# Prompt attention: maxima and sums copied to 64 columns by GpSimd and spread by two full-width products a block

## The chip, the cores and the metric

The kernel runs on one core of a Trainium2 chip. The metric is device time of one execution, in microseconds (us), as the median of several runs. Engines are called as in the profile: PE is TensorE (PEld its weight loads), DVE is VectorE, ACT is ScalarE, POOL is GpSimd, SP is SyncE, which here issues DMAs.

## The reference

One inference step of a trunk with two layers: an RWKV-7 layer and a layer of dilated sliding-window attention, each followed by a gated ConvFFN. Everything is float32. The prompt has 1024 tokens, the samples 64. What matters here is the attention of the prompt in three head groups with (window, dilation) = (128, 1), (512, 4), (2048, 16):

```python
sc = jnp.einsum('bdnqhe,bdnkhe->bdnqhk', qb, kb) * ATT_SCALE
sc = jnp.where(valid, sc, -jnp.inf)
lse = jax.nn.logsumexp(sc, axis=-1)
pr = jnp.exp(sc - lse[..., None])
o = jnp.einsum('bdnqhk,bdnkhe->bdnqhe', pr, vb)
...
wts = jax.nn.softmax(jnp.stack(lses), axis=0)
o = jnp.sum(wts[..., None] * jnp.stack(outs), axis=0)
```

So for each query and head the kernel needs, beside the weighted values, the maximum and the sum of its exponentials. They join the three groups in the end.

## The kernel before

`prompt_attention` works through 12 slots. A slot is one pair of heads (i = 0 to 3) in one head group (g = 0 to 2), in the order (0,0), (0,1), (0,2), (1,0) and so on. A slot has 8 blocks of 128 queries, and a block is handled for both heads of the pair, each with 64 channels.

The order on PE is written out by hand. The loop over a slot s has ten steps, n = 0 to 9. In step n PE issues `scores(s, n)` (for n < 8), a first part of the projections of slot s + 1 (`advance(s + 1, n, 0)`), `turn(s, n - 1)` (transposes of the exponentials), a second part of the projections (`advance(s + 1, n, 1)`) and `values(s, n - 2)`. Which pieces of the next slot's projections go into which step stands in `STEPS`: rotations rK and V products in steps 6 to 8, and in step 9 only the transposes T of V. The last slot, 11, has no next slot, so its steps hold attention alone.

`values(s, n)` writes one PSUM bank, `ps[:, 7]`: columns 0 to 127 get the weighted values (L2645 for the earlier key block, where there is one, and L2648 for the block's own), columns 128 to 255 the negated maxima, columns 256 to 383 the sums. Maxima `nm` and sums `zz` lie in SBUF with the query on the partition, one column a head. Line L2652 spreads such a column over 64 channels: its stationary operand is the column repeated 64 times (a broadcast read), its moving operand the 128 x 128 identity, its output 64 partitions x 128 queries. It is issued four times a block (2 quantities x 2 heads), each with 128 rows and 64 columns of the array. The last of them raises `nfull`; DVE then copies all 384 columns out (L2808) and raises `ntaken`.

The shapes of the array on PE around it: scores (L2618) use 64 rows and 128 columns (written 64\*128 in the profile), values and spreading 128 rows and 64 columns (128\*64), the projections (L2545, L2566), rotations (L2576), transposes of exponentials (L2630) and T in groups 0 and 1 (L2587) use 128\*128, T in group 2 (L2589) 128\*64. In float32 each product is two instructions on PE, and so two rows of a count.

The softmax of a block: DVE scales and masks (L2796), then takes the negated maximum (L2800); ACT forms the exponentials with the sum as a by-product, one head at a time (L2701), and raises `expd`; PE transposes them (L2630); ACT copies them out (L2711).

POOL in this function builds sums of weights for the projections, four additions of 128 x 512 a slot (L2524 to L2529), once the DMA has brought the slot's weights and PE has used the ones before; behind the loop it clears two regions for the sampled attention (L2531, L2533). In the slots 3, 6 and 9 DVE also joins the three groups of the previous pair (`later.merge`, L2346 to L2366, 128 x 1024 each, among them a reciprocal at L2363).

SP issues the weights of the next slots, the stores, and towards the end the loads and masks of the sampled attention (L2321, L2329, L2323). The block of `sampled_attention` begins when all engines have ended this one.

`tail` is called twice, once a layer. Its first product waits for the output weights by two semaphores.

Of the kernel before, what the change touches and what calls it, by code (L numbers as in the profile page):

```python
# [8 lines left out]
ALU = mybir.AluOpType  # L9
# [4 lines left out]
P = 128  # L14
# [42 lines left out]
    return region[:, start:start + count * width].rearrange("p (n w) -> p n w", w=width)  # L57


def tail(m, a, layer, src, kt, weights, mixed, middle, reload=None, save=None, early=None):  # L60

    nc = m.nc
    PADW = SEQ + 2 + NB * (NS + 2)
# [55 lines left out]

    with ExitStack() as ctx:  # L120
        sem = lambda n: ctx.enter_context(nc.semaphore(f"t{layer}_{n}"))
        wo_first, wo_rest = early if early is not None else (sem("wo_first"), sem("wo_rest"))
        xin = sem("xin") if reload is not None else None
        wup = [[sem(f"wup{s}{q}") for q in range(2)] for s in range(2)]
        vin = [sem(f"vec{s}") for s in range(2)]
# [87 lines left out]

        @block.sync
        def _(sp):
            if early is None:
                sp.dma_start(wot[:, 0], weights[0]).then_inc(wo_first, 16)
                sp.dma_start(wot[:, 1:KT], weights[1:KT].rearrange("n p k c -> p n k c")).then_inc(wo_rest, 16)
            if reload is not None:
                sp.dma_start(m.X, reload).then_inc(xin, 16)  # L220

            def keep_rows(f):

                sp.wait_ge(kept, f * 2 + 2)
                for q in range(2):
                    sp.dma_start(a["o_conv"][layer, f + q * FT], last2[:, 2 * (f % 2) + q, :]).then_inc(rows_out[f % 2], 16)

            for f in range(FT):
                s = f % 2
                if f == 2:  # L230
                    for b, (t0, n) in enumerate(TB):
                        sp.wait_ge(added, KT * (b + 1))
                        sp.dma_start(middle[:, :, t0:t0 + n], m.X[:, :, t0:t0 + n]).then_inc(m.x_moved, 16)
                for q in range(2):
                    if f >= 2:
                        sp.wait_ge(up, last_up(f - 2, q))
                    sp.dma_start(wt[s][q], a["wup"][layer, q * FT + f]).then_inc(wup[s][q], 16)
                if f >= 2:
                    keep_rows(f - 2)
                    sp.wait_ge(hidden, f - 1)  # L240
                sp.dma_start(vec[:, s, :], a["ffv"][layer, f]).then_inc(vin[s], 16)
            def part_in(n, q, r, dst, signal):
                sp.dma_start(dst, a["wdown"][layer, 2 * (n % 4) + q, :, r * HF:(r + 1) * HF, :]).then_inc(signal, 16)

            def keep_block(b):
                if b < 2:
                    sp.wait_ge(added, NU + KT * (b + 1))
                    rows = XIN[b]
                else:
                    if b == 3:  # L250
                        sp.wait_ge(conv, CONVS + 4)
                    sp.wait_ge(added, NU + (3 * KT if b == 2 else 3 * KT + 4))
                    rows = XS[b - 2]
                if save is not None:
                    sp.dma_start(save[:, :, DB[b]:DB[b] + PIECE], rows).then_inc(m.x_moved, 16)
                else:
                    sp.dma_start(a["o_y"][:, :, DB[b]:DB[b] + PIECE], rows).then_inc(y_out, 16)

            sp.wait_ge(up, last_up(FT - 2, 1))
            part_in(0, 0, 0, W11, a11_in)  # L260
            keep_rows(FT - 2)
            sp.wait_ge(conv, CONVS - 2)
            part_in(0, 1, 0, W21, a21_in)
            sp.wait_ge(up, at[FT - 1, 0, 2])
            part_in(0, 0, 1, W12, a12_in)
            sp.wait_ge(up, at[FT - 1, 1, 2])
            part_in(0, 1, 1, W22, a22_in)
            sp.wait_ge(m.x_moved, stored)
            sp.dma_start(m.H[:, :, HALF:T], middle[:, :, 0:HALF]).then_inc(m.x_moved, 16)
            keep_rows(FT - 1)  # L270
            for n in range(1, NDOWN):
                sp.wait_ge(product, down(n - 1, "P7"))
                part_in(n, 0, 0, W11, a11_in)
                if n == 5:
                    sp.wait_ge(m.x_moved, stored + 16)
                    sp.dma_start(hid[:, KT:2 * KT, 0:HALF], middle[:, :, HALF:T]).then_inc(m.x_moved, 16)
                sp.wait_ge(product, down(n - 1, "P5"))
                part_in(n, 1, 0, W21, a21_in)
                sp.wait_ge(sums_done, WSUMS + 4 * n)
                part_in(n, 0, 1, W12, a12_in)  # L280
                sp.wait_ge(product, down(n - 1, "P4"))
                part_in(n, 1, 1, W22, a22_in)
                if n == 5:
                    sp.wait_ge(m.x_moved, stored + 32)
                    keep_block(0)
                if n == 6:
                    keep_block(1)
                    if save is not None:
                        sp.wait_ge(m.x_moved, stored + 64)
            keep_block(2)  # L290
            keep_block(3)
            if save is not None:
                sp.wait_ge(m.x_moved, stored + 96)
            else:
                sp.wait_ge(y_out, 64)
            for s in range(2):
                sp.wait_ge(rows_out[s], FT * 16)

        @block.tensor
        def _(pe):  # L300
# [6 lines left out]
            def mixer(b, k):  # L307
                u = KT * b + k
                t0, n = TB[b]
                begun = early is not None and u < EARLY  # L310
                if early is not None:
                    pe.wait_ge(wo_first if begun else wo_rest, 16 if begun else 48)
                elif u < 2:
                    pe.wait_ge((wo_first, wo_rest)[u], 16)
                if u >= 6:
                    pe.wait_ge(taken, u - 5)
                for c in range(kt - 1 if begun else 0, kt):
                    mm = pe.matmul(m.ps[:, u % 6, 0:n], wot[:, k, c, :], src[:, c, t0:t0 + n], start=(c == 0), stop=(c == kt - 1),  # L318
                                   skip_group_check=begun)
                mm.then_inc(product, 1)  # L320
# [2048 lines left out]
def prompt_attention(m, a, scratch, later):  # L2369
# [38 lines left out]
    with ExitStack() as ctx:  # L2408
# [2 lines left out]
            sem(n) for n in ("consts", "proj", "proj_act", "proj_dve", "roped", "kv_stored"))  # L2411
        sfull, biased, maxed, expd, ptfull, pt, nfull, ntaken = (
            sem(n) for n in ("scores", "biased", "maxed", "exp", "pt_psum", "pt", "out_psum", "out"))
        sums_done, token_sums = sem("sums"), sem("token_sums")
        wl = [sem(f"wl{n}") for n in range(3)]
        bt = lambda n: m.big[:, n * T:(n + 1) * T]
        Q, K, V, R, QP, COS, SIN = [bt(0), bt(4)], [bt(1), bt(5)], bt(2), bt(3), bt(6)[:, 0:SEQ], bt(20), bt(21)
# [1 line left out]
        o = 3 * SEQ  # L2419
        masks = m.tmp[:, o:o + 3 * P].rearrange("p (n k) -> p n k", n=3)  # L2420
        rot = m.tmp[:, o + 384:o + 512]
        nm = m.tmp[:, o + 512:o + 528].rearrange("p (i h) -> p i h", i=8)
        zz = m.tmp[:, o + 528:o + 544].rearrange("p (i h) -> p i h", i=8)
        Vt = m.tmp[:, o + 544:o + 544 + 8 * P].rearrange("p (n j) -> p n j", n=8)
        wt = [tiles(m.w, n * D, KT, P) for n in range(3)]
        S2, S3, S4 = tiles(m.lanes, 0, 4, P), tiles(m.w, 3 * D + 2048, 4, P), tiles(m.tmp, o + 1568, 4, P)
# [89 lines left out]

        @block.gpsimd
        def _(pool):
            for s in range(NSLOT):
                if s:  # L2520
                    wait_piece(pool, s - 1, ("P3", 1))
                for t in range(2):
                    pool.wait_ge(wl[t], 16 * (s + 1))
                pool.tensor_tensor(S3, A[0][0], A[1][0], ALU.subtract)  # L2524
                pool.tensor_tensor(A[1][0], A[1][0], A[1][1], ALU.add)
                pool.drain()
                pool.tensor_tensor(S2, A[1][0], A[0][0], ALU.subtract).then_inc(sums_done, 1)
                pool.drain()
                pool.tensor_tensor(S4, A[0][1], S2, ALU.subtract).then_inc(sums_done, 1)  # L2529
            wait_piece(pool, NSLOT - 1, ("V", 2))  # L2530
            pool.memset(later.blocks, 0.0).then_inc(later.zeroed, 1)  # L2531
            pool.wait_ge(later.zeroed, 1)
# [3 lines left out]
        def _(pe):  # L2536
# [97 lines left out]
            def values(s, n):  # L2634
# [12 lines left out]
                for h in range(2):  # L2647
                    pe.matmul(ps[64 * h:64 * h + 64, 0:P], Vt[:, n, 64 * h:64 * h + 64], PT[n % 2][:, h, 1, :],  # L2648
                              start=(b4 is None), stop=True)
                for q, t in ((1, nm), (2, zz)):  # L2650
                    for h in range(2):
                        mm = pe.matmul(ps[64 * h:64 * h + 64, q * P:(q + 1) * P],  # L2652
                                       t[:, n, h:h + 1].broadcast_to([P, 64]), m.ident[:, :], start=True, stop=True)
                mm.then_inc(nfull, 1)

            for n in range(10):
# [365 lines left out]
def hybrid_step(nc, a):  # L3022
# [6 lines left out]
    with ExitStack() as ctx:  # L3029
        m = Machine(nc, ctx)  # L3030
        rwkv_inputs(m, a, rkv)
        with ExitStack() as first:
            wo_first, wo_rest = (first.enter_context(nc.semaphore(n)) for n in ("wo_first", "wo_rest"))
            rwkv_core(m, a, rkv, wo_first, wo_rest)
            tail(m, a, 0, m.H, KT, a["wo"], tiles(m.big, 0, KT, T), middle[0], reload=a["xT"], save=kept, early=(wo_first, wo_rest))
        with ExitStack() as both:
            later = Samples(m, a, qkv, both)
            prompt_attention(m, a, qkv, later)
            sampled_attention(m, a, later)
        tail(m, a, 1, tiles(m.big, AO_TILE * T, AP_, T), AP_, a["at_wo"], m.H, middle[1], reload=kept)  # L3040


# [168 lines left out]
```

## Time and profile before

| | us |
|---|---|
| median of 3 runs | 4000.13 (4000.05 to 4004.37) |
| profiled execution | 4001.5 |
| its span, first to last instruction | 3999.7 |
| PE busy in the span | 3677.7 (92%) |
| DVE / ACT / POOL busy | 2264.1 / 819.9 / 740.1 |

The profiled execution is 1.8 us longer than its span, and 1.4 us over the median. The prompt attention lies from about 2130 to 2925 us of the span. In rows of the trace, a time at the beginning is the start in us from the span's start, then comes the busy time in us of a group of consecutive instructions. PE's instructions are pipelined: a product begins before the one before it has ended, so the distance between starts is what one costs.

### The profile page before, as it was taken

What the parts mean: (1) busy time and instruction counts of PE and PEld (TensorE: products, weight loads), DVE (VectorE), ACT (ScalarE), POOL (GpSimd) and SP (SyncE); (2) the same over time, 40 slices, a digit from 0 to 9 for tenths busy, and PEclk for the clock granted to TensorE, in tenths of its full rate; (3) what the DMA queues carried; (4) which work ended last, traced back from release to release, by engine and by line L of the source; (5) the groups of instructions that cost most, each with busy time, mean ns of one, the idle gap of its engine ahead of it and who ended that gap; (6) DMA issues with size and microseconds to landing.
All of it is one profiled execution on the core that took longest, in us unless ns stands there. A gap on an engine that the chain in (4) does not pass through costs nothing. (4 is left out here: it accounts for less than half of the span.)

```text
span 3999.7 us, 80774 instructions
## 1 busy us (share of the span) xinstructions
PE 3677.7 (92%) x35376; PEld 2856.0 (71%) x35376; DVE 2264.1 (57%) x3406; ACT 819.9 (20%) x1870; POOL 740.1 (19%) x504
## 2 busy tenths in 40 slices
PE   7999688888799999999997999999967999999997
PEld 4888466666656888877785777777644688887886
DVE  8441577676447566672636446565555666667253
ACT  6110334433222011110111222222223110111000
POOL 1221000000012222213432101010102222221343
PEclk9999899999999999999998999999988999999999
DMA  2221211100121111112322111111383111112232
GB/s 81 85 76 69 66 36 41 35 29 29 44 93 51 44 44 44 44 45 95 113 70 80 39 46 39 46 41 46 125 297 138 46 44 38 40 44 74 87 104 79
DMA packets 119046, 268.80 MB, mean 67 GB/s; under 512 B 38056, under 2 KB 59944, under 8 KB 116264
## 3 DMA queue, kind: packets, MB, share of 16 engines
q1 hardware_dynamic: 118696, 263.63, 19.0%
q8 instruction: 281, 4.60, 0.5%
q14 instruction: 69, 0.57, 0.0%
HBM read 214.64 MB, written 48.95 MB: 66 GB/s over the span
## 5 line engine op out<-in xcount | busy, mean ns | idle before, releaser
L373 PE MATMUL ps<-sb_h,sb_w 128*128 128x272 f32 x1672 | 408.1, 392 | 1.4 <-ACT sb_tmp L522 1.4
L373 PEld LDWEIGHTS ps<-sb_h,sb_w 128*128 128x128 f32 x1672 | 317.5, 190 | 67.6 <-issue 2.3
L373 PE MATMUL ps<-sb_x,sb_w 128*128 128x272 f32 x1216 | 291.1, 392 | 0.0
L373 PEld LDWEIGHTS ps<-sb_x,sb_w 128*128 128x128 f32 x1216 | 231.0, 190 | 47.6
L430 PE MATMUL ps<-sb_big,sb_w 128*128 128x272 f32 x1056 | 251.9, 397 | 2.5 <-issue 1.3
L430 PEld LDWEIGHTS ps<-sb_big,sb_w 128*128 128x128 f32 x1056 | 202.9, 192 | 46.8 <-issue 4.3
L725 DVE SCALAR_TENSOR_TENSOR sb_big<-sb_tmp,sb_big 128x1024 f32<-128x1024 f32 (+1 forms) x176 | 203.3, 1155 | 13.2
L2545 PE MATMUL ps<-sb_h,sb_w 128*128 128x384 f32 (+1 forms) x576 | 186.9, 468 | 0.0
L1409 PE MATMUL ps<-sb_x,sb_w 128*128 128x272 f32 x768 | 183.8, 392 | 0.0
L343 PE MATMUL ps<-sb_h,sb_w 128*128 128x384 f32 (+1 forms) x576 | 177.1, 469 | 3.9 <-DVE sb_tmp L700 2.1
L1409 PEld LDWEIGHTS ps<-sb_x,sb_w 128*128 128x128 f32 x768 | 145.9, 190 | 30.1
L430 PE MATMUL ps<-sb_x,sb_w 128*128 128x272 f32 x672 | 160.2, 394 | 0.0
L752 DVE TENSOR_TENSOR sb_big<-sb_big,ps 128x544 f32<-128x544 f32 x38 | 27.4, 722 | 233.4 <-PE ps L373 233.3
L343 PEld LDWEIGHTS ps<-sb_h,sb_w 128*128 128x128 f32 x576 | 109.1, 190 | 70.7 <-issue 5.6
L2755 DVE TENSOR_TENSOR sb_big<-sb_big,ps 128x272 f32<-128x272 f32 x120 | 52.6, 438 | 185.0 <-PE ps L2566 179.9
L2701 ACT ACTIVATE sb_w<-sb_w,sb_tmp 128x128 f32<-128x128 f32 (+1 forms) x192 | 84.9, 443 | 333.4 <-DVE sb_tmp L2800 333.4
L725 DVE SCALAR_TENSOR_TENSOR sb_w<-sb_tmp,sb_w 128x1024 f32<-128x1024 f32 (+1 forms) x176 | 143.3, 814 | 13.2
L430 PEld LDWEIGHTS ps<-sb_x,sb_w 128*128 128x128 f32 x672 | 128.5, 191 | 26.8
L373 PE MATMUL ps<-sb_x,sb_lanes 128*128 128x272 f32 x608 | 145.5, 392 | 0.0
L373 PE MATMUL ps<-sb_x,sb_tmp 128*128 128x272 f32 x608 | 145.5, 392 | 0.0
L2566 PE MATMUL ps<-sb_x,sb_w 128*128 128x272 f32 x576 | 145.0, 398 | 0.0
L2545 PEld LDWEIGHTS ps<-sb_h,sb_w 128*128 128x128 f32 x576 | 106.9, 190 | 53.1
(396 smaller groups left out, 7067.6 us busy)
## 6 DMA issues: line engine op xcount, KB each, us to landing
sb_w<-wup SPq DMA_DIRECT2D x88, 512.0 KB, 4.1
sb_w<-wdown SPq DMA_DIRECT2D x48, 704.0 KB, 4.1
sb_w<-wqkv SPq DMA_DIRECT2D x36, 512.0 KB, 3.5
sb_w<-wrkv SPq DMA_DIRECT2D x24, 512.0 KB, 5.5
sb_tmp<-wdown SPq DMA_DIRECT2D x16, 704.0 KB, 4.0
sb_x<-kT SPq DMA_DIRECT2D x10, 1024.0 KB, 12.0
rkv_scratch<-sb_big SPq DMA_DIRECT2D x18, 544.0 KB, 6.5
sb_big<-vc SPq DMA_DIRECT2D x9, 1024.0 KB, 11.6
```

What stands on the lines that cost most here:

```text
L343: mm = pe.matmul(m.ps[:, 3 * q + b, 0:n], wt[f % 2][q][:, k, :], m.H[:, k, t0:t0 + n], start=(k == 0), stop=(k == KT - 1))
L373: mm = pe.matmul(m.ps[:, 2 * HOME[f][p] + e, 0:PIECE], w, rhs[:, k, e * PIECE:(e + 1) * PIECE], start=(k == 0 and p not in ("P2", "P3")), ...
L430: mm = pe.matmul(m.ps[:, BANK[n, p], 0:PIECE], lhs[:, k, :], rhs(k), start=(k == 0 and p not in ("P2", "P3")), stop=(k == HF - 1), skip_gr ...
L725: ins = dve.scalar_tensor_tensor(out=out, in0=tap(j), scalar=cw(j), in1=out, op0=ALU.mult, op1=ALU.add)
L752: dve.tensor_tensor(U2, U2, pair_ps(f, "P6"), ALU.add).then_inc(parted, 1)
L1409: mm = pe.matmul(m.ps[:, bank, 0:PIECE], lhs[:, k, :], rhs(k), start=(k == 0 and p not in ("P2", "P3")), stop=(k == 3), skip_group_check=True)
L2545: mm = pe.matmul(m.ps[:, ring(s, p), 0:w], wt[t][:, k, :], m.H[:, k, t0:t0 + w], start=(k == 0), stop=(k == KT - 1))
L2566: mm = pe.matmul(m.ps[:, ring(s, p), 0:PIECE], lhs[:, k, :], rhs[:, k, :], start=(k == 0 and n not in ("P2", "P3")), stop=(k == 3), skip_g ...
L2701: ins = act.activation(SM[n % 2][:, h, lo:2 * P], SM[n % 2][:, h, lo:2 * P], ACT.Exp, bias=nm[:, n, h:h + 1], accum_out=zz[:, n, h:h + 1])
L2755: dve.tensor_tensor(out, kept, ps, op).then_inc(ptd, 1)
```

## The change

POOL gets a new operation for each block, `widen(s, n)`: it reads the four columns of the block (two maxima, two sums, now side by side in `nmzz`), multiplies by ones, and writes 4 x 64 = 256 columns into one half of a double buffer `wide`, in a region of the attention's output that is written later. It waits for `expd` of the block and, for the buffer, for `nfull` of two blocks before, and raises `widened`.

In `values`, the four products of 64 columns become two of 128 columns (maxima of both heads, sums of both heads), and PE waits for `widened` ahead of them.

POOL's order changes: sums of weights of slots 0 and 1 come first, then eight `widen` a slot, with the sums of weights of slot s + 2 between `widen(s, 6)` and `widen(s, 7)`. The two clearings come behind the last `widen`. The two semaphores of `tail`'s output weights are now shared by both layers (the second waits for higher counts).

```diff
-        nm = m.tmp[:, o + 512:o + 528].rearrange("p (i h) -> p i h", i=8)
-        zz = m.tmp[:, o + 528:o + 544].rearrange("p (i h) -> p i h", i=8)
+        nmzz = m.tmp[:, o + 512:o + 544].rearrange("p (i q) -> p i q", i=8)
+        nm, zz = nmzz[:, :, 0:2], nmzz[:, :, 2:4]
+        wide = tiles(bt(AO_TILE + AP_ - 1), 0, 2, 4 * 64)
...
-            for s in range(NSLOT):
+            def weight_sums(s):
                 if s:
                     wait_piece(pool, s - 1, ("P3", 1))
...
+            def widen(s, n):
+                pool.wait_ge(expd, 8 * s + n + 1)
+                if 8 * s + n >= 2:
+                    pool.wait_ge(nfull, 8 * s + n - 1)
+                pool.tensor_tensor(wide[:, n % 2, :].rearrange("p (q e) -> p q e", q=4), nmzz[:, n, :].unsqueeze(2).broadcast_to([P, 4, 64]),
+                                   m.ones[:, 0:64].unsqueeze(1).broadcast_to([P, 4, 64]), ALU.mult).then_inc(widened, 1)
+
+            weight_sums(0)
+            weight_sums(1)
+            for s in range(NSLOT):
+                for n in range(8):
+                    widen(s, n)
+                    if n == 6 and s + 2 < NSLOT:
+                        weight_sums(s + 2)
             wait_piece(pool, NSLOT - 1, ("V", 2))
...
-                for q, t in ((1, nm), (2, zz)):
-                    for h in range(2):
-                        mm = pe.matmul(ps[64 * h:64 * h + 64, q * P:(q + 1) * P],
-                                       t[:, n, h:h + 1].broadcast_to([P, 64]), m.ident[:, :], start=True, stop=True)
+                pe.wait_ge(widened, 8 * s + n + 1)
+                for q in range(2):
+                    mm = pe.matmul(ps[:, (q + 1) * P:(q + 2) * P], wide[:, n % 2, q * P:(q + 1) * P], m.ident[:, :], start=True, stop=True)
                 mm.then_inc(nfull, 1)
...
-                    pe.wait_ge((wo_first, wo_rest)[u], 16)
+                    pe.wait_ge((wo_first, wo_rest)[u], (32, 64)[u])
```

## Rows read from the trace of the kernel before

**Rows 1.** Busy time of each engine in three stretches (slots 3, 5, 11).
```profile
core 0: us, PE busy (x) PEld busy (x) DVE busy (x) ACT busy (x) POOL busy (x), PEclk, DMA share, GB/s
...
2375.00:2441.00 66.00, 62.85 (x396) 46.65 (x395) 55.07 (x67) 18.61 (x52) 6.96 (x4) 0.99 0.11 39
...
2508.00:2568.00 60.00, 60.00 (x330) 42.64 (x330) 26.50 (x52) 13.90 (x50) 5.30 (x4) 1.00 0.12 40
...
2896.00:2925.00 29.00, 16.21 (x146) 10.09 (x144) 13.13 (x25) 10.36 (x42) 0.39 (x1) 0.82 0.58 174
```

**Rows 2.** Lines L2652 and L1358: durations in ns (min/median/max) and forms.
```profile
L2652 PE MATMUL ps<-sb_ident,sb_tmp x768: 272/273/421, 2201.4 to 2916.2; 128*64 128x128 f32 x192
...
L1358 PEld LDWEIGHTS ps<-sb_ident,sb_small x20: 180/238/338, 15.8 to 40.5; 128*128 128x128 f32 x16, 32*128 32x128 f32 x4
```

**Rows 3.** Timeline of PE, end of one step (slot 5, block 2).
```profile
2536.19 0.44 PE L2648 MATMUL ps<-sb_w,sb_tmp 128*64 128x128 f32 x4
2536.46 0.61 PE L2652 MATMUL ps<-sb_ident,sb_tmp 128*64 128x128 f32 x8
2536.99 0.69 PE L2618 MATMUL ps<-sb_big 64*128 64x128 f32 x4
```

**Rows 4.** Timeline of PE and PEld: full-width spreading in the RWKV layer.
```profile
39.26 1.16 PE L1358 MATMUL ps<-sb_ident,sb_small 128*128 128x128 f32 x8
...
39.26 0.97 PEld L1358 LDWEIGHTS ps<-sb_ident,sb_small 128*128 128x128 f32 x8 [0.41 <-DVE sb_big L1242]
```

**Rows 5.** Timeline of PE and PEld: half-width, then full-width (slot 5, block 5).
```profile
2558.71 0.61 PE L2652 MATMUL ps<-sb_ident,sb_tmp 128*64 128x128 f32 x8
...
2559.25 0.30 PEld L2576 LDWEIGHTS ps<-sb_big,sb_tmp 128*128 128x128 f32 x2 [0.17 <-issue]
```

**Rows 6.** Timeline of PE: half-width, then half-width (slot 10, block 6).
```profile
2892.65 0.61 PE L2652 MATMUL ps<-sb_ident,sb_tmp 128*64 128x128 f32 x8
2893.08 0.77 PE L2589 MATMUL ps<-sb_ident,sb_big 128*64 128x128 f32 x10
```

**Rows 7.** POOL's addition nearest in size to the copy: busy us, mean ns of one.
```profile
L961 POOL TENSOR_TENSOR sb_x<-sb_big,sb_w 128x272 f32<-128x272 f32 x24 | 21.7, 931 | 33.9 <-DVE sb_w L810 33.9
```

**Rows 8.** Timeline, slot 5: POOL's sums of weights, and blocks 4, 7.
```profile
2547.24 1.26 POOL L2524 TENSOR_TENSOR sb_w<-sb_w 128x512 f32<-128x512 f32 x1 [58.79 <-DMA sb_w<-wqkv]
...
2551.29 1.55 POOL L2529 TENSOR_TENSOR sb_tmp<-sb_w,sb_lanes 128x512 f32<-128x512 f32 x1 [0.16 <-issue]
...
2550.34 0.61 PE L2652 MATMUL ps<-sb_ident,sb_tmp 128*64 128x128 f32 x8
...
2566.56 0.64 PE L2652 MATMUL ps<-sb_ident,sb_tmp 128*64 128x128 f32 x8
```

**Rows 9.** Timeline of DVE and POOL in slot 3, and PE's wait there.
```profile
2418.92 0.44 DVE L2763 TENSOR_TENSOR sb_big<-ps,sb_big 128x272 f32<-128x272 f32 x1 [0.68 <-PE ps L2576]
2419.16 1.27 POOL L2527 TENSOR_TENSOR sb_lanes<-sb_w 128x512 f32<-128x512 f32 x1
2419.28 1.73 DVE L2768 TENSOR_TENSOR sb_big<-sb_big 128x544 f32<-128x544 f32 x1
...
2427.73 0.71 DVE L2768 TENSOR_TENSOR sb_big<-sb_big 128x544 f32<-128x544 f32 x1
...
2439.40 0.44 PE L2645 MATMUL ps<-sb_w,sb_tmp 128*64 128x128 f32 x4 [3.07 <-DVE sb_tmp L2808]
```

**Rows 10.** PE's waits for other engines, 2186 to 2896 us: us, times, longest.
```profile
PE ps L2645 <- DVE sb_tmp L2808: 6.1, 2, 3.1
PE ps L2645 <- DVE sb_big L2808: 3.4, 1, 3.4
```

**Rows 11.** Timeline at the end: last spreading, SP's issues, PE's next work.
```profile
2904.82 18.78 SPq L2329 DMA_DIRECT2D sb_h<-c_smask  x12
...
2915.85 0.64 PE L2652 MATMUL ps<-sb_ident,sb_tmp 128*64 128x128 f32 x8
...
2925.18 2.74 PE L2863 MATMUL ps<-sb_ident,sb_h 128*64 128x128 f32 x12 [8.70 <-PEq L2408]
```

More of the change, by code:

```diff
@@ L57, in tiles, with tail @@
     return region[:, start:start + count * width].rearrange("p (n w) -> p n w", w=width)
-def tail(m, a, layer, src, kt, weights, mixed, middle, reload=None, save=None, early=None):
+def tail(m, a, layer, src, kt, weights, mixed, middle, mixer_in, reload=None, save=None, early=False):
     nc = m.nc
@@ L121, in tail @@
         sem = lambda n: ctx.enter_context(nc.semaphore(f"t{layer}_{n}"))
-        wo_first, wo_rest = early if early is not None else (sem("wo_first"), sem("wo_rest"))
+        wo_first, wo_rest = mixer_in
         xin = sem("xin") if reload is not None else None
@@ L215, in _ @@
         def _(sp):
-            if early is None:
+            if not early:
                 sp.dma_start(wot[:, 0], weights[0]).then_inc(wo_first, 16)
@@ L309, in mixer @@
                 t0, n = TB[b]
-                begun = early is not None and u < EARLY
-                if early is not None:
+                begun = early and u < EARLY
+                if early:
                     pe.wait_ge(wo_first if begun else wo_rest, 16 if begun else 48)
                 elif u < 2:
-                    pe.wait_ge((wo_first, wo_rest)[u], 16)
+                    pe.wait_ge((wo_first, wo_rest)[u], (32, 64)[u])
                 if u >= 6:
@@ L2413, in prompt_attention @@
             sem(n) for n in ("scores", "biased", "maxed", "exp", "pt_psum", "pt", "out_psum", "out"))
-        sums_done, token_sums = sem("sums"), sem("token_sums")
+        sums_done, token_sums, widened = sem("sums"), sem("token_sums"), sem("widened")
         wl = [sem(f"wl{n}") for n in range(3)]
@@ L3031, in hybrid_step @@
         rwkv_inputs(m, a, rkv)
[L3032 to L3035, printed above, removed]
+        wo_first, wo_rest = (ctx.enter_context(nc.semaphore(n)) for n in ("wo_first", "wo_rest"))
+        rwkv_core(m, a, rkv, wo_first, wo_rest)
+        tail(m, a, 0, m.H, KT, a["wo"], tiles(m.big, 0, KT, T), middle[0], (wo_first, wo_rest), reload=a["xT"], save=kept, early=True)
         with ExitStack() as both:
@@ L3039, in hybrid_step @@
             sampled_attention(m, a, later)
-        tail(m, a, 1, tiles(m.big, AO_TILE * T, AP_, T), AP_, a["at_wo"], m.H, middle[1], reload=kept)
+        tail(m, a, 1, tiles(m.big, AO_TILE * T, AP_, T), AP_, a["at_wo"], m.H, middle[1], (wo_first, wo_rest), reload=kept)
 def _tiled(w):
```

## Prediction

> **What bounds the kernel now.** I read the busy time by stretches first. From slot 0 to slot 10 PE is the pace: in slot 5, say, it is busy 60.00 of 60.00 us, at a granted clock of 1.00 (the level of 2.4 GHz), while DVE has 26.50 and POOL 5.30 [rows 1]. The list of PE's waits for other engines says the same: 9.5 us in 710, in three places, all for DVE's copy L2808 ahead of L2645 [rows 10]. These three are the slots in which DVE joins the groups; there it is busy 55.07 of 66 us [rows 1, 9]. Slot 11 is another matter. PE is busy 16.21 of 29 us, its last spreading ends by 2916.5, and its next work begins at 2925.18 after 8.70 us of idleness, when SP has got through the issues that began at 2904.82 and lasted 18.78 us [rows 1, 11]. So what PE gains or loses in slots 0 to 10 goes into the end, and what it loses in slot 11 is covered by up to 8.7 us.
>
> **What the spreading costs now.** The list of costly groups would mislead: 768 instructions of 273 ns look like a large sum [rows 2]. The timeline gives the distance of starts. Eight instructions of L2652 take 0.61 us, of which 0.27 is the length of the last one, so the eight starts lie within 0.34 us [rows 3, 2]. One product streams 128 columns, and full-width passes of the same size, spreading the same way (L1358), start one each 0.112 us: the eight loads take 0.97 us, the last one's own length is 0.18 to 0.19, so seven distances are 0.78 or 0.79 [rows 4, 2]. The products' 1.16 us less the last one's 0.27 is 0.89, seven distances and a first load of 0.10 to 0.11. Eight half-width passes one after another would need seven such distances, 0.78 us, where 0.34 are seen. So the two heads' passes run side by side in the two halves of the array, and L2652 costs four distances of 0.11, or 0.44 us. The change also needs four passes (two products of two), full-width, of 0.112: **0.45 us**. The array's work stays what it is; half of the instructions carried nothing.
>
> The Trainium skill, TensorEngine Tiling (Array Packing), section Tiling Modes, lists 128x64 as two independent tiles that load and multiply in parallel, which the rows above bear out. It also says that changing the tiling mode (not just the tile) drains TensorE. That rule speaks against this change; its price is not on the page, and I take it from rows.
>
> **The added switch of shape.** Before, L2645, L2648 and L2652 are all 128\*64 and follow without a break: L2648's last pass starts at 2536.19 + 0.44 - 0.27 = 2536.36, L2652's first at 2536.46, 0.10 later [rows 3]; L2652 to L2589, same shape, likewise: 2892.65 + 0.34 = 2892.99 to 2893.08 [rows 6]. Where the shape changes from 128\*64 to 128\*128, the last pass starts at 2558.71 + 0.34 = 2559.05 and the next load only at 2559.25: 0.20 us, and the first product follows its load by another 0.11 [rows 5, 4]. That is 0.31 us from pass to pass against 0.10, so such a switch costs **0.205 us**. A switch into 128\*64 costs less for its shorter load: four passes of L2648 take 0.44, so 0.17 to the last start, of which 0.11 is a distance and 0.06 the load [rows 3]; 0.20 + 0.06 - 0.11 = 0.15 us.
>
> Whether this adds to the block depends on what follows `values` in PE's order. The switch out of 128\*64 was paid behind L2652 already.
> - Next are scores (64\*128), in the blocks 0 to 4 and 7: the old switch stays (2536.46 + 0.34 to 2536.99 is 0.19, as out of any shape [rows 3]) and the new one comes on top. 6 blocks x 11 slots = 66 x 0.205 = 13.5 us.
> - Next is 128\*128 work, block 5 (the rotation rK) and block 6 where the next slot is of group 0 or 1: the switch only moves ahead of the spreading. 11 + 7 = 18 x 0.01 = 0.2 us.
> - Next is 128\*64 work, block 6 ahead of a slot of group 2 (4 times): there was no switch [rows 6] and there will be two, 0.205 + 0.15 = 0.35; 4 x 0.35 = 1.4 us.
> - Slot 11: up to 8 x 0.2 = 1.6 us, covered as said [rows 11]; without the cover it would be added. POOL's two clearings move behind the last `widen`, to about 2914, which leaves them 11 us before PE's next work.
>
> Sum on PE: **15.1 us**. No row shows a wait ahead of a change of shape that costs less than the drain; if the next load could be made ready, the 0.09 us of drain alone would stay (66 x 0.09 + 4 x 0.18 = 7 us). If the new wait or the wider load costs another 0.1 us, it is 66 x 0.305 + 4 x 0.45 = 22 us. I take the middle, because rows 5 are the same pair of shapes.
>
> **POOL.** The copy is 128x256. POOL needs 931 ns for 128x272 [rows 7], so I take 0.9 us; a repeated read could make it cheaper or dearer (0.5 to 1.5). In slots 0 to 10 it has the time from the end of `values(n-2)` to the spreading of `values(n)`, two steps. The shortest stretch is that of block 7: it may start after `values(5)`, about 2559.3, and is wanted at 2566.56, 7.2 us later [rows 5, 8]. Ahead of it on POOL lie the moved sums of weights, which begin after `widen(6)`, about 2551.9 (block 4's spreading ends at 2550.95), and take 5.6 us (2547.24 to 2552.84), so to 2557.5, before `values(5)` [rows 8]. Their own reader comes in the next slot. Hidden: 0.
>
> **DVE beside POOL.** In the slots 3, 6 and 9 DVE is late and PE waits 3.07 us for it [rows 9]. Its chain there goes back to 2418.92, its last wait for PE. In it an addition (L2768) beside a POOL operation takes 1.73 us, and alone 0.71 [rows 9]. The sums of weights now fall about 6 us later, inside this chain, and copies are added. One to two more such meetings a slot, 1.0 us each, less 0.2 us of a switch that falls into the time PE waits anyway: I take 0.8 x 3 = **2.4 us**, between 0 and 9. The Trainium skill, SBUF — State Buffer, section SBUF: two separate sides, says that GpSimd and a VectorE operation with two SBUF inputs hold a shared port pair for a whole instruction; the trace agrees (1.73 against 0.71). Elsewhere DVE has over 30 us of room a slot. The semaphores of `tail` and the layout of `nmzz` cost nothing: the same waits and the same sizes.
>
> Sum: 15.1 + 2.4 = 17.5 us. The profiled execution would go from 4001.5 to 4019.0; against the median of 4000.1 this is **4017.6**. Bounds: 4000.1 + 7 = 4007, and 4000.1 + 22 + 9 = 4031. A measurement of this kernel tells about 0.2% (8 us) from no change.
>
> **Rivals.**
> - *The half-width passes do not overlap* (faster). If each took its own distance, L2652 would cost 8 x 0.11 = 0.88 us and the change would save 0.44. That decides as soon as the saving is over the 0.205 of the switch: 66 x (0.205 - 0.44) + 18 x (0.01 - 0.44) + 4 x (0.35 - 0.44) = -23.6 us, so 3976 to 3979 with DVE's part. Against it speak the eight starts in 0.34 us [rows 3]; for it only that starts in a trace could be noted early. Chance 0.06.
> - *The switch is free or absorbed* (no change). PE is busy all the time in slot 5 [rows 1], but a busy PE is not PE at its peak. If another engine set the pace, or dropping half of the instructions paid for the drain, the time would be 4000 to 4008. Against it: the PE waits are 9.5 us in all [rows 10]. Chance 0.09.
> - *The copy comes late* (much slower). It decides from about 7 us a copy: at 9 us POOL would need 8 x 9 + 6 = 78 us a slot, against 64, or 11 x 14 = 150 us, so about 4150. Between them lies a POOL that waits behind DVE's long operations in three slots, 3 x 7 = 21 us, 4038. Against it speak 0.93 us for a larger addition [rows 7] and the seven us of room. Chance 0.05.
>
> **How the numbers follow.** The forecast has 0.80. Its range is 4007 to 4028: the upper bound of 4031 needs both costs at their highest, so I cut it a little. The rest is the rivals. Faster 0.06; same 0.10 (the absorbed case and the lowest edge of the forecast); slower 0.84.
>
> **What would show it.** In the profile after: four full-width instructions a block instead of eight, at distances of 0.11; 0.20 us between the last start of L2648's passes and the load of the spreading, with idle time put down to "issue"; the same 0.19 ahead of the scores; in slots 0 to 10 steps longer by 0.2 us where scores follow, and unchanged at block 5; POOL's copies at 0.5 to 1.5 us, ended some us before PE wants them; PE's waits for DVE in slots 3, 6 and 9 about as long or 1 us longer; PE idle ahead of 2925 shorter by a little over 1 us. Wrong would be: starts of the half-width passes that did not show their cost, a PE that waits for POOL, or a DVE that loses over 3 us a joining slot.

## The result: 0.48% slower

The changed kernel takes 4024.25 us (median of 8 runs, 4016.75 to 4033.91), the kernel before 4004.61 (8 runs, 4000.05 to 4013.28). The ratio is 1.0048, 95% interval 1.0037 to 1.0059: 19 us slower, from 15 to 24. The forecast was 17.5 us. The profiled execution has a span of 4025.3 us, 25.6 more than before.

Two profiles differ by some us outside of the change: the first values product of slot 0 starts 5.3 us later than before, and in other kernels of this study, whose earlier part is the same, from 5.4 us earlier to 5.6 later. So I measure the stage itself: from the first values product of slot 0 to that of slot 11. First the kernel before, then the one after, from the timelines of PE (start, busy us):

```profile
2201.09 0.44 PE L2648 MATMUL ps<-sb_w,sb_tmp 128*64 128x128 f32 x4
...
2900.58 0.44 PE L2648 MATMUL ps<-sb_w,sb_tmp 128*64 128x128 f32 x4
```
```profile
2206.44 0.44 PE L2664 MATMUL ps<-sb_w,sb_tmp 128*64 128x128 f32 x4
...
2921.71 0.70 PE L2664 MATMUL ps<-sb_w,sb_tmp 128*64 128x128 f32 x4
```

The stage went from 699.49 to 715.27 us: **15.8 us more**, in 88 blocks.

Where they lie is plain in the end of one step, slot 5, block 2, the same place as [rows 3]. Timeline of PE, then of PEld, of the kernel after:

```profile
2550.32 0.44 PE L2664 MATMUL ps<-sb_w,sb_tmp 128*64 128x128 f32 x4
2550.69 0.71 PE L2668 MATMUL ps<-sb_ident,sb_big 128*128 128x128 f32 x4
2551.33 0.69 PE L2634 MATMUL ps<-sb_big 64*128 64x128 f32 x4
```
```profile
2550.32 0.20 PEld L2664 LDWEIGHTS ps<-sb_w,sb_tmp 128*64 128x64 f32 x4 [0.36 <-issue]
2550.69 0.52 PEld L2668 LDWEIGHTS ps<-sb_ident,sb_big 128*128 128x128 f32 x4 [0.17 <-issue]
2551.33 0.30 PEld L2634 LDWEIGHTS ps<-sb_big 64*128 64x128 f32 x4
```

The same loads before:

```profile
2536.19 0.20 PEld L2648 LDWEIGHTS ps<-sb_w,sb_tmp 128*64 128x64 f32 x4 [0.36 <-issue]
2536.35 0.47 PEld L2652 LDWEIGHTS ps<-sb_ident,sb_tmp 128*64 128x64 f32 x8
```

From the values to the scores it is 1.01 us, against 2536.99 - 2536.19 = 0.80 in [rows 3]. The values are as long as they were (0.44). The spreading's first load starts 0.37 us behind their first, where it had started 0.16 behind. From that load to the scores it is 0.64 us in both kernels: four passes instead of eight leave the spreading no shorter. The gap of 0.17 put down to "issue" is new. At block 5, where 128\*128 work follows, PEld shows the same gap ahead of the spreading and none behind it, where [rows 5] had it:

```profile
2573.19 0.20 PEld L2664 LDWEIGHTS ps<-sb_w,sb_tmp 128*64 128x64 f32 x4 [0.36 <-issue]
2573.56 0.52 PEld L2668 LDWEIGHTS ps<-sb_ident,sb_big 128*128 128x128 f32 x4 [0.17 <-issue]
2574.00 0.30 PEld L2592 LDWEIGHTS ps<-sb_big,sb_tmp 128*128 128x128 f32 x2
```

Taken over all slots 0 to 10, the distance from block to block grew by 0.20 us behind each of the blocks 0 to 4 and by 0.01 us behind block 5, without an exception. Behind block 7 it grew by 0.20 or 0.21 in seven slots, by 0.43 in slot 10, and by 1.45, -0.31 and -0.43 in the joining slots 3, 6 and 9, where it is the granted clock that differs (see the part on the prediction, DVE beside POOL). In all 96 blocks the load of the spreading starts 0.20 us (at the lower clock 0.35) behind the last start of the values.

POOL's copies and PE's waits, from the groups by form and the list of waits (2192 to 2918 us):

```profile
L2536 POOL TENSOR_TENSOR sb_big<-sb_tmp,sb_ones 128x256 f32<-128x256 f32 x96 | 66.1, 689 | 632.4 <-PE ps L2668 445.1 <-ACT sb_w L2716 187.3
```
```profile
PE ps L2661 <- DVE sb_tmp L2823: 6.3, 2, 3.1
PE ps L2661 <- DVE sb_big L2823: 3.5, 1, 3.5
```

A copy takes 0.69 us in the mean, and PE never waits for POOL. Its waits for DVE in the three joining slots are 9.8 us, against 9.5 in [rows 10].

### The profile page after: what moved, and what is told of

Same layout as the page of the kernel before. It is cut to its first block and busy times, and to the rows that moved or that the text cites. A ratio compares the mean times of both kernels' runs of the same rounds, so it can differ in the third digit from the quotient of the medians.

```text
span 4025.3 us, 80196 instructions
## 1 busy us (share of the span) xinstructions
PE 3707.0 (92%) x34992; PEld 2872.0 (71%) x34992; DVE 2261.9 (56%) x3406; ACT 820.8 (20%) x1870; POOL 806.7 (20%) x600
## 5 line engine op out<-in xcount | busy, mean ns | idle before, releaser
L373 PEld LDWEIGHTS ps<-sb_h,sb_w 128*128 128x128 f32 x1672 | 317.5, 190 | 67.6 <-issue 2.3
L2536 POOL TENSOR_TENSOR sb_big<-sb_tmp,sb_ones 128x256 f32<-128x256 f32 x96 | 66.1, 689 | 632.4 <-PE ps L2668 445.1
L343 PEld LDWEIGHTS ps<-sb_h,sb_w 128*128 128x128 f32 x576 | 109.1, 190 | 70.6 <-issue 5.6
## 6 DMA issues: line engine op xcount, KB each, us to landing
sb_x<-kT SPq DMA_DIRECT2D x10, 1024.0 KB, 11.9
```

What stands on the lines that cost most here:

```text
L343: mm = pe.matmul(m.ps[:, 3 * q + b, 0:n], wt[f % 2][q][:, k, :], m.H[:, k, t0:t0 + n], start=(k == 0), stop=(k == KT - 1))
L373: mm = pe.matmul(m.ps[:, 2 * HOME[f][p] + e, 0:PIECE], w, rhs[:, k, e * PIECE:(e + 1) * PIECE], start=(k == 0 and p not in ("P2", "P3")), ...
L2536: pool.tensor_tensor(wide[:, n % 2, :].rearrange("p (q e) -> p q e", q=4), nmzz[:, n, :].unsqueeze(2).broadcast_to([P, 4, 64]), m.ones[:, ...
```

## Experiments

Two theories stood at the start. **The switch**: the array's work is the same four pass distances, and all the cost is an added change of the array's shape, 0.205 us. **The rivals**: POOL's copies, their wait or their meetings with DVE; or full-width products that are dear in themselves. Each ratio is to runs of the kernel before taken beside it. The stage difference is taken from the profiles as above; "a step" is the growth of the distance from block to block where scores follow.

| kernel | ratio to before, 95% | stage, us | a step, us |
|---|---|---|---|
| changed kernel | 1.0048 (1.0037 to 1.0059) | +15.8 | +0.20 |
| e1_half_from_wide | 1.0004 (0.9993 to 1.0015) | -0.3 | 0.00 |
| e3_half_then_full | 1.0048 (1.0030 to 1.0066) | +15.0 | +0.20 |
| e4_full_then_half | 1.0069 (1.0050 to 1.0088) | +27.2 | +0.35 |
| e5_full_first | 1.0008 (0.9998 to 1.0019) | +2.0 | +0.01 |
| e6_spread_once | 0.9919 (0.9904 to 0.9934) | -35.1 | -0.44 |
| e7_heads_apart | 1.0010 (0.9999 to 1.0021) | +4.1 | +0.05 |
| f1_one_head | 1.0003 (0.9994 to 1.0013) | 0.0 | -0.01 |
| f2_one_half | 1.0080 (1.0064 to 1.0095) | +29.9 | +0.43 |
| e8_transposed_first | 0.9971 (0.9960 to 0.9983) | -11.9 | -0.22 |
| e9_transposed_last | 0.9982 (0.9971 to 0.9992) | -6.9 | -0.07 |

**All of the change but the width** (against the changed kernel):

```diff
                 for q in range(2):
-                    mm = pe.matmul(ps[:, (q + 1) * P:(q + 2) * P], wide[:, n % 2, q * P:(q + 1) * P], m.ident[:, :], start=True, stop=True)
+                    for h in range(2):
+                        mm = pe.matmul(ps[64 * h:64 * h + 64, (q + 1) * P:(q + 2) * P],
+                                       wide[:, n % 2, q * P + 64 * h:q * P + 64 * h + 64], m.ident[:, :], start=True, stop=True)
```

> Everything of the change except the width: POOL copies and reorders as in the changed kernel, PE waits for the copy, but spreads with four products of 64 columns out of the copy. Theory (the added switch of array shape, 0.205 us a block): no added switch, so 0 us on PE; within 3 us of the kernel before, about 4004 where that is 4004. Rival 1 (POOL's copies, their wait, or DVE's meetings with POOL carry the cost): still 15 to 20 us slower than before. Rival 2 (the cost comes with full-width products as such): also as before. In the trace: eight instructions of the spreading a block within 0.61 us, directly behind the values.

Measured: 1.0004, stage -0.3 us, no step changed where scores or rotations follow. POOL's 96 copies, its new order, PE's wait and the read of a copied column instead of a repeated one cost nothing that the ratio or the stage shows; only PE's three waits for DVE grow, from 9.5 to 10.4 us. Rival 1 is out.

**One full-width product, behind (shown) or ahead of the half-width ones:**

```diff
-                for q in range(2):
-                    mm = pe.matmul(ps[:, (q + 1) * P:(q + 2) * P], wide[:, n % 2, q * P:(q + 1) * P], m.ident[:, :], start=True, stop=True)
+                for h in range(2):
+                    mm = pe.matmul(ps[64 * h:64 * h + 64, 1 * P:2 * P],
+                                   wide[:, n % 2, 0 * P + 64 * h:0 * P + 64 * h + 64], m.ident[:, :], start=True, stop=True)
+                mm = pe.matmul(ps[:, 2 * P:3 * P], wide[:, n % 2, 1 * P:2 * P], m.ident[:, :], start=True, stop=True)
```

> The maxima are spread by two half-width products, then the sums by one full-width product. Theory (switches): four passes' distances as in both kernels, one added switch as in the changed kernel: +15 us against before (+0.37%), steps longer by 0.20 us where scores follow, unchanged at block 5. Rival (a full-width product costs about 0.10 us more by itself, so two cost 0.2): half, +7 to 8 us.

> The same three products as in the kernel with half-width first, in the other order: the maxima by one full-width product, then the sums by two half-width ones. Theory (switches): two added switches a block wherever the next work comes, 0.205 + 0.15 = 0.355 us; 88 blocks x 0.355 = 31 us slower than before (+0.78%). Rival (a full-width product costs by itself): the same as with the half-width ones first, +7 to 8 us.

Timeline of PE in slot 5, block 2, half-width first and then full-width first:

```profile
2549.55 0.44 PE L2664 MATMUL ps<-sb_w,sb_tmp 128*64 128x128 f32 x4
2549.82 0.39 PE L2668 MATMUL ps<-sb_ident,sb_big 128*64 128x128 f32 x4
2550.14 0.49 PE L2670 MATMUL ps<-sb_ident,sb_big 128*128 128x128 f32 x2
2550.56 0.69 PE L2634 MATMUL ps<-sb_big 64*128 64x128 f32 x4
```
```profile
2545.24 0.44 PE L2664 MATMUL ps<-sb_w,sb_tmp 128*64 128x128 f32 x4
2545.61 0.49 PE L2667 MATMUL ps<-sb_ident,sb_big 128*128 128x128 f32 x2
2546.03 0.44 PE L2669 MATMUL ps<-sb_ident,sb_big 128*64 128x128 f32 x4
2546.39 0.69 PE L2634 MATMUL ps<-sb_big 64*128 64x128 f32 x4
```

The same three products take 1.01 us from values to scores in the one order and 1.15 in the other, where before had 0.80. One full-width product with one added switch costs as much as two with one (0.20 each), and two added switches cost 0.35. So the cost goes by switches, not by full-width products; their prices are the forecast's 0.205 and 0.15. The stage of the second order is 27.2 instead of 31 us: in the slots 3, 6 and 9 PE waits for DVE 7.2 us instead of 9.5, and so takes a part of its growth out of waiting; these three grew by 4.8 us, not 8.5.

**Full-width products ahead of the values:**

```diff
                 ps = m.ps[:, 7, :]
                 b4 = before(g, n)
+                pe.wait_ge(widened, 8 * s + n + 1)
+                for q in range(2):
+                    pe.matmul(ps[:, (q + 1) * P:(q + 2) * P], wide[:, n % 2, q * P:(q + 1) * P], m.ident[:, :], start=True, stop=True)
...
-                pe.wait_ge(widened, 8 * s + n + 1)
-                for q in range(2):
-                    mm = pe.matmul(ps[:, (q + 1) * P:(q + 2) * P], wide[:, n % 2, q * P:(q + 1) * P], m.ident[:, :], start=True, stop=True)
```

> The changed kernel with the two full-width products moved ahead of the block's values, so that they follow 128*128 work and the switch to 128*64 comes behind them. Theory (switches): no added switch except at block 7 behind the transposes for a group-2 slot (4 times, 0.355 us): 2 us over before, about 4006 where that is 4004. Rival (full-width products, POOL's copies or the wait cost by themselves): +15 to 20 us as in the changed kernel.

Measured: 1.0008, stage +2.0 us, 0.01 a step. Nothing else differs from the changed kernel than the place of the two products with their wait (so that the values now raise `nfull`), and the stage is 13.8 us shorter. The total is as forecast, its parts are not quite: from block 6 to block 7 the growth is 0.25 to 0.33 us ahead of the four group-2 slots, but 0.16 too in the slots 2, 5 and 8, and the joining slots are 0.7 shorter together.

**What the spreading costs, and why.** The first of four kernels leaves it out behind slot 0's first block, and POOL's copies with it:

```diff
+                if s == 0 and n == 0:
+                    for q in range(2):
+                        for h in range(2):
+                            pe.matmul(ps[64 * h:64 * h + 64, (q + 1) * P:(q + 2) * P],
+                                      nmzz[:, n, 2 * q + h:2 * q + h + 1].broadcast_to([P, 64]), m.ident[:, :], start=True, stop=True)
...
-                for q in range(2):
-                    mm = pe.matmul(ps[:, (q + 1) * P:(q + 2) * P], wide[:, n % 2, q * P:(q + 1) * P], m.ident[:, :], start=True, stop=True)
```

The second swaps the two loops of the first experiment:

```diff
-                for q in range(2):
-                    for h in range(2):
+                for h in range(2):
+                    for q in range(2):
```

The last two were made after those results. They keep half-width products with repeated reads, as before, and no copies, but behind the first block spread only head 0 (shown), or both heads into the lower half (`range(2)` in place of the last `range(1)`):

```diff
-                pe.wait_ge(widened, 8 * s + n + 1)
+                every = s == 0 and n == 0
                 for q in range(2):
-                    mm = pe.matmul(ps[:, (q + 1) * P:(q + 2) * P], wide[:, n % 2, q * P:(q + 1) * P], m.ident[:, :], start=True, stop=True)
+                    for h in range(2) if every else range(1):
+                        o = 64 * h if every else 0
+                        mm = pe.matmul(ps[o:o + 64, (q + 1) * P:(q + 2) * P],
+                                       nmzz[:, n, 2 * q + h:2 * q + h + 1].broadcast_to([P, 64]), m.ident[:, :], start=True, stop=True)
```

> Leaves out the spreading in all blocks but the first of each third... of the first slot only (all later blocks are copied out with whatever the bank holds), and POOL's copies with it. Prices the spreading. Theory (four distances of 0.11 us a block): 87 x 0.44 = 38 us faster than before, about 3966. Rival (eight passes of 0.11 us one after another, so that two full-width products would halve it): 76 us faster, about 3928.

> Four half-width products out of the copy as in the run that leaves the width, but in the order head 0 maxima, head 0 sums, head 1 maxima, head 1 sums, so neighbours share a half of the array. Theory (the eight passes are cheap because neighbours run side by side in the two halves, and PE begins its products in order): at least three more distances of 0.11 us, 88 x 0.33 = 29 us slower than before; in the trace eight starts over some 0.7 us instead of 0.34. Rival (a half-width pass of 128 columns is cheap in itself, 0.05 us): no difference to before.

> No POOL copies, half-width products as before; but behind the first block only head 0 is spread: two half-width products, four passes, all in the lower half of the array. Leaves out the spreading of head 1. Theory (passes cost 0.11 us each within one half, and the two halves run at the same time): four distances of 0.11 us a block as before, no gain, 0 +- 3 us. Rival, raised by the order that changed nothing (a half-width pass costs only 0.055 us wherever it lies): four passes fewer a block, 0.22 x 87 = 19 us faster.

> All four half-width products of the kernel before, but both heads written to the lower half, head 1 over head 0, so that all eight passes lie in one half of the array. Leaves out the output of head 0's spreading. Theory (two halves side by side): eight distances of 0.11 us, 0.44 us more a block, 88 x 0.44 = 38 us slower than before (+0.95%), a little less where PE waits for DVE in three slots. Rival (half-width passes cheap anywhere): 0 us.

Leaving it out saves 0.44 us a step, 35.1 us in the stage: that is the price of the spreading before, and it is four distances, not eight. The order head by head broke my expectation: 0.05 us a step instead of 0.33. That left room for a pass that is cheap wherever it lies, so I tried the halves themselves. Timeline of PE in slot 5, block 2, of heads apart, one head, and one half:

```profile
2532.92 0.66 PE L2669 MATMUL ps<-sb_ident,sb_big 128*64 128x128 f32 x8
```
```profile
2540.47 0.60 PE L2665 MATMUL ps<-sb_ident,sb_tmp 128*64 128x128 f32 x4
```
```profile
2557.63 1.04 PE L2665 MATMUL ps<-sb_ident,sb_tmp 128*64 128x128 f32 x8
```

Four passes in one half take 0.60 us, as long as eight in two halves (0.61 in [rows 3]); eight in one half take 1.04, which is four distances of 0.11 more. Half of the instructions left out gained nothing (1.0003); all eight put on one half cost 0.80%. (In the stage that is 29.9 us and not 38, because the joining slots grew by 3.0 where 24 blocks by 0.43 are 10.3.) So the two halves do run side by side, and this is shown now by runs and not only by starts in a trace. Why the order of the program hardly matters is not settled: neighbours in the order head by head share a half, and yet the eight starts lie within 0.66 - 0.27 = 0.39 us. The trace does not name the half of an instruction, but its single records in this place form two rows: starts at 2532.92, 2533.03, 2533.14 and 2533.25, and at 2532.93, 2533.09, 2533.20 and 2533.31. Read as one row for each half, both halves run from the beginning, at their own distance of 0.11 us, whatever stands between them in the program.

**A shorter spreading.** A transpose of the copied columns gives the same result, and is one instruction on PE where a float32 product is two (x2 in the rows below, x4 for the two products). Behind the values it looks as shown; in the other kernel wait and transposes stand ahead of the values:

```diff
                 for q in range(2):
-                    mm = pe.matmul(ps[:, (q + 1) * P:(q + 2) * P], wide[:, n % 2, q * P:(q + 1) * P], m.ident[:, :], start=True, stop=True)
+                    mm = pe.transpose(ps[:, (q + 1) * P:(q + 2) * P], wide[:, n % 2, q * P:(q + 1) * P], m.ident[:, :])
```

> The two full-width products become transposes of the copied columns (one pass of PE each in float32 where a product has two), ahead of the values. Computes the same. Theory: two distances of 0.11 us instead of four, no added switch: 88 x 0.22 = 19 us saved, less 2 for the four places behind 128*64 work: 17 us faster than before (-0.43%), about 3987. Rival (the copies and their wait cost by themselves): at or over before.

> The same two transposes, behind the values as in the changed kernel. Theory: two distances saved, one switch added: 66 x (0.205 - 0.22) + 18 x (-0.22) + 4 x (0.355 - 0.22) = -4.4 us, about 4000 where before is 4004, and 13 to 15 us behind the same transposes put first. Rival (no cost of the switch): the same as with the transposes first.

Timeline of PE in slot 5, block 2, transposes last (the two alone), then transposes first:

```profile
2530.81 0.44 PE L2668 MATMUL ps<-sb_ident,sb_big 128*128 128x128 f32 x2
```
```profile
2531.87 0.38 PE L2661 MATMUL ps<-sb_ident,sb_big 128*128 128x128 f32 x2
2532.18 0.44 PE L2667 MATMUL ps<-sb_w,sb_tmp 128*64 128x128 f32 x4
2532.55 0.69 PE L2634 MATMUL ps<-sb_big 64*128 64x128 f32 x4
```

Transposes first are the fastest kernel here that leaves nothing out, 0.29% under the kernel before (0.17 to 0.40%), and last they still gain 0.18%. A step shrinks by 0.22 and by 0.07 us; the difference of 0.15 is less than the switch of 0.20, because the first load of a transpose is exposed for 0.06 us only: last, the two take 0.44 us, of which 0.27 is the last one's length and 0.11 the distance. In the stage the two places differ by 5.0 us, not by the 13 to 15 expected: 6.6 in the eight other slots, taken back in part by the joining ones.

First, the stage gained 11.9 us and not 17. The eight other slots gained 12.5, as forecast; all that is missing lies in the joining slots, which are no shorter than before (207.5 us together from values to values, before 206.9). PE arrives earlier there and idles longer, 12.7 us in three places ahead of a block's first product, where the kernel before waits 9.5 us for DVE's copy. The profile puts these waits down to "issue", but in all three places PE's first product starts 0.1 us behind the end of DVE's copy of the block before. In slot 3, with transposes first:

```profile
2435.25 0.56 DVE L2823 COPY sb_tmp<-ps 128x384 f32<-128x384 f32 x1
2435.88 0.29 PEld L2661 LDWEIGHTS ps<-sb_ident,sb_big 128*128 128x128 f32 x2 [4.26 <-issue]
```

So it is DVE that holds these slots. What a shorter DVE would give was not tried.

## Why the prediction was right, point by point

- *PE is the pace in slots 0 to 10*: right. What was added a block came out at the end of the stage, 15.8 us of it.
- *Half-width passes run side by side, and the spreading costs 0.44 us*: right, measured as 0.44 a step by leaving it out. The rival of the other side (two full-width products halve it) fell with the result, and with the kernel that spreads one head only.
- *A switch costs 0.205 us into 128\*128 and 0.15 into 128\*64*: measured 0.20 and, by the second order, 0.35 for both, so 0.15 for the second.
- *By what follows*: the steps ahead of scores by 0.20, right, but for block 7 of the joining slots and of slot 10, as told above. Block 5 by 0.01, right. Block 6 ahead of a group-2 slot: I had 0.35, measured 0.29 or 0.30. Block 6 ahead of the other slots: I had 0.01, and it is 0.2 in the slots 2, 5 and 8. The step that failed there is that I counted only PE's own work. Timeline of slot 5, block 6 of the kernel after:

```profile
2579.56 0.71 PE L2668 MATMUL ps<-sb_ident,sb_big 128*128 128x128 f32 x4
2580.30 0.81 DVE L2823 COPY sb_big<-ps 128x384 f32<-128x384 f32 x1 [2.66 <-PE ps L2668]
2581.26 0.44 PE L2664 MATMUL ps<-sb_w,sb_tmp 128*64 128x128 f32 x4
```

  And before:

```profile
2565.36 0.82 DVE L2808 COPY sb_big<-ps 128x384 f32<-128x384 f32 x1 [2.44 <-PE ps L2652]
...
2566.32 0.44 PE L2648 MATMUL ps<-sb_w,sb_tmp 128*64 128x128 f32 x4
```

  The values of block 7 start 0.15 us behind the end of DVE's copy of block 6 after and 0.14 before, so they wait for it in both kernels, and `nfull` of block 6 is what the switch delays; that the switch behind it is gone does not help. Three times 0.2 us. Why it is 0.29 and not 0.35 ahead of group 2 was not taken apart.
- *DVE beside POOL in the joining slots*: mis-sized. I took 2.4 us, bounds 0 to 9, from meetings of 1.0 us. With POOL's part alone (the first experiment) the three waits for DVE went from 9.5 to 10.4 us, so the meetings cost 0.3 us a slot; without copies and with the old order of POOL (one head only) they were 9.6. In the changed kernel they are 9.8: the switch of 0.2 that falls into the waiting time is taken off, as I had said. Net that is 0.3 us in the three slots where I had 2.4. The 1.73 us against 0.71 in [rows 9] is itself from a meeting of the kernel before, and a meeting moved is not a meeting added.

  I overlooked what comes behind these waits. Stretches from block 7's values in the slots 3, 6 and 9 to the next slot's first, before and after:

```profile
2439.60:2457.90 18.30, 18.30 (x90) 13.88 (x86) 5.82 (x12) 5.17 (x18) 0.00 (x0) 0.91 0.18 67
2633.30:2652.30 19.00, 19.00 (x88) 14.53 (x85) 5.76 (x12) 5.18 (x18) 0.00 (x0) 0.87 0.17 63
2827.50:2846.70 19.20, 19.20 (x90) 14.62 (x86) 5.70 (x12) 5.17 (x18) 0.00 (x0) 0.86 0.16 63
```
```profile
2450.50:2470.30 19.80, 19.80 (x87) 14.86 (x84) 5.64 (x13) 5.18 (x18) 1.22 (x2) 0.85 0.16 61
2649.50:2668.20 18.70, 18.70 (x86) 14.17 (x82) 5.80 (x12) 5.18 (x18) 1.22 (x2) 0.91 0.17 64
2847.30:2866.10 18.80, 18.80 (x86) 14.24 (x83) 5.80 (x12) 5.18 (x18) 1.23 (x2) 0.91 0.17 64
```

  PE is busy throughout, and the granted clock, 1.00 in slot 5 [rows 1], is 0.85 to 0.91: it is down at the beginning of each stretch (in slot 3 after, 0.50 up to 2456 us and 1.00 from 2458). The length follows the clock: 18.3 us at 0.91 and 19.0 or 19.2 at 0.87 and 0.86 before, 18.7 or 18.8 at 0.91 and 19.8 at 0.85 after. Hence the +1.45, -0.31 and -0.43 behind block 7 (together 0.7, where three switches are 0.6: in this pair the clock nearly cancels out), and hence a stage of the first experiment that is 0.3 us shorter with longer waits (its slot 6 has 0.91 here, and 18.3 us). Differences of this kind, of up to 1.8 us a joining slot, are in every stage figure above.

  So the whole stage grew by 15.8 us where PE's part alone was forecast as 15.1, and that the sum of 17.5 lies nearer to the 19 measured than 15.1 does is luck: the term that brings it there measured 0.3. The 3 us between the stage and the ratio are inside the ratio's interval and not explained further.
- *The copy is hidden*: right. I took 0.9 us, a copy of repeated columns took 0.61 at best and 0.69 in the mean, and PE never waited for POOL.
- *Slot 11 is covered*: right in the profile, but with far less room than I said. From the stretches between the first and the last values product of slot 11, before and after, and PE's next work after:

```profile
2900.60:2915.60 15.00, 12.54 (x117) 8.12 (x117) 9.14 (x18) 7.25 (x31) 0.00 (x0) 0.89 0.86 235
```
```profile
2921.70:2943.00 21.30, 19.86 (x89) 12.88 (x89) 9.53 (x17) 7.12 (x31) 6.67 (x8) 0.50 0.64 179
```
```profile
2926.55 18.86 SPq L2329 DMA_DIRECT2D sb_h<-c_smask  x12
...
2947.00 0.61 PE L2878 MATMUL ps<-sb_ident,sb_h 128*64 128x128 f32 x2 [2.13 <-PEq L2408]
```

  Eight switches would be 1.6 us. Slot 11 grew by 6.3, because the granted clock there was 0.50 (1.2 GHz) throughout instead of 0.89: four passes of the values take 0.70 us there and 0.44 before (the rows of 2921.71 and 2900.58 above). PE's idle time ahead of the next block, 8.70 us in [rows 11], is 2.13. It still ends with SP's issues: from the first values product of slot 11 to PE's next work it is 25.3 us against 24.6 before, within the 23.6 to 26.0 of the other kernels. So the profile shows no loss. A run in which the cover falls short was not seen, though one full-width product behind the half-width ones left only 1.16 us. POOL's clearings began at 2939.9, 7 us ahead of PE's next work, where I had 11.

The Trainium skill's rule in TensorEngine Tiling (Array Packing), Tiling Modes, that a change of mode drains TensorE, agrees with the 0.20 us between the last start in one shape and the first load in the next; these runs price it.

## What to carry to other kernels

Count a group of PE instructions by the distance of their starts, not by their number or their mean length: products in different halves of the array share one distance, and merging them into one wide product takes away instructions and no time. Before merging, look at the array shape of what stands on either side; a new shape between two others costs a drain and an exposed load each time (0.20 us here), and the same lines put next to work of their own shape cost 0.01. If such a product only copies or spreads, see whether a transpose does it in half of the passes.

## What the runs showed of the hardware that was not expected

- The order of half-width products hardly matters: eight passes with neighbours in the same half took 0.66 us against 0.61, where starts in the program's order would need at least 0.9 (six distances of 0.11 and the last one's 0.27). The Trainium skill, TensorE: Matmul & The Clock Gate, Part 3, says that matmuls keep strict order in start and end; by that rule the run should have been 0.3 us a block slower. Whether PE or an earlier stage reorders is open.
- The granted clock of slot 11, which has the same work in all kernels but the spreading, was 0.89 before and with half-width products out of the copy, heads together or apart (15.0, 15.1 and 15.2 us), and 0.50 in the changed kernel and with one full-width product behind or ahead of the half-width ones (21.3, 21.3 and 22.7 us). But it was 0.93 with both full-width products ahead of the values (14.8 us), 1.00 with one head only, 0.85 with one half, 0.52 with the spreading left out, and 0.50 and 0.53 with transposes first and last. So neither the width nor POOL's copies sort them. Each figure is one profile, and whether a kernel has the same clock there in every execution was not tried. In all of them PE comes from work without gaps into a slot in which it idles between short pieces (12.54 of 15.00 us busy before). What tips it was not tried.
- In the joining slots, behind PE's wait for DVE, the granted clock is down for some us although PE is busy without a gap again. From block 7's values to the next slot it was 0.86 to 0.91 in the kernel before (waits of 3.1 to 3.4 us), 0.83 or 0.84 in all three slots with transposes first (4.1 to 4.5 us), and 1.00 in the slots 6 and 9 with all passes in one half (2.5 and 2.1 us), where the stretch took 17.5 us instead of 19.0 and 19.2. So such a wait costs more than its own length.
- A POOL product of two repeated reads, 128x256, took 0.61 us at best, less than its size suggested from the 0.93 of 128x272 in [rows 7].
